# MLP up products of a hybrid encoder step: moving operand read in alternating pieces of 4 columns

## The reference

```python
h = _rmsnorm(x, norm2_g) * (1.0 + sc2) + sh2
x = x + g2 * (jnp.square(jax.nn.relu(h @ w_up)) @ w_down)
```

## Time and profile before

| what | us |
|---|---|
| median of 2 runs | 3328.43 |
| the two runs | 3326.7, 3330.15 |
| span of the profiled execution, first to last instruction | 3325.1 |
| TensorE busy in it | 3224.1 (97%) |
| VectorE busy | 1696.0 (51%) |
| ScalarE busy | 984.5 (30%) |
| GpSimd busy | 957.8 (29%) |

### The profile page before, as it was taken

One profiled execution on the slowest core, in us unless ns is written; L12 is line 12 of the kernel. 1 busy time (PEld: TensorE's weight loads), 2 busy tenths in 40 slices (PEclk: granted clock), 3 DMA queues, 4 the chain that ended last, 5 costly groups with the idle time before them and its releaser, 6 DMA issues.

```text
span 3325.1 us, 50329 instructions
## 1 busy us (share of the span) xinstructions
PE 3224.1 (97%) x19286; PEld 2894.2 (87%) x19286; DVE 1696.0 (51%) x3073; ACT 984.5 (30%) x1770; POOL 957.8 (29%) x690
## 2 busy tenths in 40 slices
PE   6999999899999999999999999999999999999998
PEld 3988897566799999999988879966678999999997
DVE  4746273674495555555573544156546633333335
ACT  3132222574451111111232313147635311111112
POOL 1312332221232333333332214212213233333332
PEclk8999999999999999999999999999999999999999
DMA  5512476535112222222222114563321011111112
GB/s 213 180 47 95 156 238 218 125 91 139 33 59 85 85 76 76 88 82 82 83 64 73 35 50 176 190 172 76 76 66 45 27 51 44 44 45 50 44 44 72
DMA packets 135351, 307.07 MB, mean 92 GB/s; under 512 B 53789, under 2 KB 74341, under 8 KB 131729
## 3 DMA queue, kind: packets, MB, share of 16 engines
q1 hardware_dynamic: 93584, 224.39, 23.4%
q10 hardware_dynamic: 41600, 80.44, 6.9%
HBM read 240.14 MB, written 57.90 MB: 90 GB/s over the span
## 4 chain that ended last, share of the span: by engine, by line
PE 90%; DVE 4%; SPq 2%; ACT 1%; ACTq 1%; issue 1%; DMA 1%; DVEq 0%
PE ps L1387 22%; PE ps L1358 19%; PE ps L1299 9%; PE ps L1232 8%; PE ps L1022 6%; PE ps L1212 5%; PE ps L1078 4%; PE ps L1169 3%; PE ps L1276 3%; PE ps L1004 2%; PE ps L1046 1%; DVE tn L2053 1%; PE ps L1334 1%; DVE h_lo L2066 1%; DVE x L2238 1%; PE ps L1113 1%
## 5 line engine op out<-in xcount | busy, mean ns | idle before, releaser
L768 POOL CAST w_hi<-raw 128x1024 fp32r<-128x1024 f32 x212 | 229.5, 1082 | 1862.5 <-PEq L1393 447.3
L2238 DVE SCALAR_TENSOR_TENSOR x<-ps,mod,x 128x352 f32<-128x352 f32 (+2 forms) x768 | 353.6, 489 | 431.5 <-PE ps L1387 351.5
L1387 PE MATMUL ps<-act_hi,w_hi 128*128 128x352 f32 x1536 | 496.0, 323 | 0.0
L1387 PE MATMUL ps<-act_hi,w_lo 128*128 128x352 f32 x1536 | 492.6, 321 | 0.0
L1387 PE MATMUL ps<-act_lo,w_hi 128*128 128x352 f32 x1536 | 492.1, 320 | 0.0
L1358 PE MATMUL ps<-h_hi,w_hi 128*128 128x352 f32 x1344 | 433.5, 323 | 0.0
L1875 ACT ACTIVATE relu_b<-ps,consts 128x352 f32<-128x352 f32 x192 | 106.4, 554 | 1103.5 <-PE ps L1358 1084.3
L1358 PE MATMUL ps<-h_hi,w_lo 128*128 128x352 f32 x1344 | 430.8, 320 | 0.0
L1358 PE MATMUL ps<-h_lo,w_hi 128*128 128x352 f32 x1344 | 430.4, 320 | 0.0
L1299 PE MATMUL ps<-pT,vb 128*128 128x512 f32 (+5 forms) x1080 | 401.3, 461 | 0.0
L2302 DVE TENSOR_REDUCE pm<-ps 128x1 f32<-128x512 f32 (+4 forms) x468 | 251.2, 548 | 243.3 <-PE ps L1169 158.8
(11 more groups left out here) (223 smaller groups left out, 6112.3 us busy)
## 6 DMA issues: line engine op xcount, KB each, us to landing
raw<-in_w SPq DMA_DIRECT2D x212, 512.0 KB, 3.6
ada_next<-in_w_ada SPq DMA_DIRECT2D x48, 512.0 KB, 4.2
ada_w<-in_w_ada SPq DMA_DIRECT2D x24, 512.0 KB, 5.9
kb<-scr_k SPq DMA_DIRECT2D x36, 328.0 KB
kb<-scr_k SPq DMA_DIRECT2D x120, 82.0 KB
qb<-scr_q SPq DMA_DIRECT2D x36, 264.0 KB
ada_nat<-in_w_ada_first SPq DMA_DIRECT2D x8, 1024.0 KB, 20.5
qb<-scr_q SPq DMA_DIRECT2D x120, 66.0 KB
```

The costliest lines, as they stand in the source:

```text
L768: pool.tensor_copy(hi, raw[:, uc % 2, 0:width]).then_inc(pool_hi, 1)
L1387: last = mm(ps[:, i % 6, 0:GW], w[:, k * 256 + o * 128:k * 256 + o * 128 + 128], (act_lo if low else act_hi)[:, k * T + g * GW:k * T + (g ...
L2238: last = v.scalar_tensor_tensor(xs, ps[:, bank, a - g * GW:b - g * GW], gs, xs, ALU.mult, ALU.add)
```

## The change

A constant STRAND = 4 is new. In `up`, the moving operand of each matmul, 352 contiguous columns, is seen as two halves a of 176 columns, each 44 pieces b of 4 columns c, and is read in the order b, a, c: four columns of the first half, four of the second, the next four of the first, and so on. The output is written through a pattern of the same order (b, a, c) over the bank's first 352 columns, which is one consecutive run of addresses. So the sum of input column a * 176 + b * 4 + c stands at b * 8 + a * 4 + c. The relu of `evict` reads PSUM in pieces that put the columns back and writes relu_b in the old order; it does so for the tiles of `up` only, and those of `up_first` are made and read as before.

```diff
--- before.py
+++ after.py
@@ -36,6 +36,7 @@
 PHASES = 5
 RET, OUT0, PROJ, ATT, MLP = range(PHASES)
 PRIME = 3
+STRAND = 4
 
 
 def rows(t):
@@ -1355,8 +1356,10 @@
                             pe.wait_ge(up_relu, n * 12 + (i - 6 + 1))
                         for k in range(KB):
                             for w, low in PASSES:
-                                last = mm(ps[:, i % 6, 0:GW], w[:, b % 2, k * 128:(k + 1) * 128],
-                                          (h_lo if low else h_hi)[:, k * T + g * GW:k * T + (g + 1) * GW],
+                                last = mm(ps[:, i % 6, 0:GW].rearrange("p (b a c) -> p b a c", a=2, c=STRAND),
+                                          w[:, b % 2, k * 128:(k + 1) * 128],
+                                          (h_lo if low else h_hi)[:, k * T + g * GW:k * T + (g + 1) * GW].rearrange(
+                                              "p (a b c) -> p b a c", a=2, c=STRAND),
                                           start=(k == 0 and w is w_hi and not low), stop=(k == KB - 1 and low == 1))
                         last.then_inc(up_ps, 1)
                         if g == 0:
@@ -1872,7 +1875,12 @@
                     act.wait_ge(sq_kept, n * 12 + (i - 1))
                 else:
                     act.wait_ge(up_lo, n * 12 + 1)
-                A(relu_b[:, i % 2, :], ps[:, UP_BANK[first][i], 0:GW], ACT.Relu, bias=zero).then_inc(up_relu, 1)
+                if first:
+                    A(relu_b[:, i % 2, :], ps[:, UP_BANK[first][i], 0:GW], ACT.Relu, bias=zero).then_inc(up_relu, 1)
+                else:
+                    A(relu_b[:, i % 2, :].rearrange("p (a b c) -> p a b c", a=2, c=STRAND),
+                      ps[:, UP_BANK[first][i], 0:GW].rearrange("p (b a c) -> p a b c", a=2, c=STRAND), ACT.Relu,
+                      bias=zero).then_inc(up_relu, 1)
                 act.wait_ge(up_relu, n * 12 + (i + 1))
                 A(act_hi[:, b * T + g * GW:b * T + (g + 1) * GW], relu_b[:, i % 2, :], ACT.Square, bias=zero).then_inc(up_hi, 1)
```

## The result

The changed kernel takes 3357.08 us (two runs, 3356.68 and 3357.48) against 3328.43 us: ratio 1.0086, 95% interval 1.0069 to 1.0104. That is no change by the 2% bound, and inside the stated range, but it is a real loss of 29 us where none was forecast.

The account below looks back on a forecast made before the run. TensorE's own products, busy 97% of the span, were taken as the bound. The parts summed 0 + 0 + 0 on the 3325.1 us span, with the median 3.3 us above it: 3328 us, range 3279 to 3475 for 8 in 10.

Parts of the forecast that it names:

- The bound and the place: TensorE's products bound the kernel; only the step of L1358, 159.0 ns, or a wait opening between products can change the time.
- the wait at the turn: From up to down, a slower relu has 2.0 us of cover before down's products wait; 0 on the path.
- part 1 of the sum: Moving read of the up products in pieces of 4: taken as 0, ends -50 us and +947 us.
- the likeliest case: No change beyond some ns a product, of either sign: chance 0.73, own range 3310 to 3350 us.
- The prediction's first sign: In the profile after, a chunk's chain must again read 45.8 us for 288 products of L1358.
- its bound for being wrong: The prediction is wrong if L1358's step leaves 159 ns by more than 16 ns, or a wait opens at the turn.
- A step before the sum: From L1169's contiguous reads: a column costs about one cycle, so the 12.3 ns above 146.7 is a charge per product.
- A smaller misreading: The two times, 3326.7 and 3330.15 us, were taken to lie 1.6 and 5.1 us above the execution's span of 3325.1.
- Rival A: Each of 87 jumps stalls the moving read one cycle: step 195 ns, 146 us more, 3475 us; chance 0.11.
- Rival B: The 12.3 ns is the moving read clashing with the next weight load; two slow streams avoid it: to 3279 us; chance 0.06.
- C: The relu reading pieces becomes the bound, if past 2.6 us; at 3.6 us it adds 14 us; no chance given.
- D: The pieces merge into one run, so the operand's order is not what the instruction reads; called impossible, no price.

Follow-up runs that it names:

- evict_only: Up products read as in the kernel before, only the relu behind them reads PSUM in pieces of 4; 3328.48 us, ratio 0.9997 to the kernel before.

## Why the prediction was right and wrong

**The bound and the place** were right. TensorE's step is all that moved; the eviction was free (evict_only), and the wait at the turn didn't open even where the square became 0.33 us longer. By the price of a ns, 4.03 us, 7.8 ns make 31.4 us, and the chunks of the chain add up to just that.

**The step that made the forecast miss** is part 1 of the sum, the moving read, "I take 0, the value that the nearest row has". It measured 7.8 ns a product, 31.4 us, and nothing else in the sum moved. The row was read rightly as far as a stream can tell: 384 columns cost 175.5 ns in three pieces and in one, and L1212's 177.2 ns, with pieces further apart, lies 1.7 ns above. But it was too far in shape. 7.8 ns lies inside the ends that were given, -12.3 and 235, and the likeliest case's own range, 3310 to 3350, allowed 5 ns on a product; it was too narrow by 7 us. The prediction's first sign, 45.8 us for 288 products, was missed by 2.2 us, while its bound for being wrong, 16 ns, was twice the change that came. The prediction thought in jumps only, and priced a jump. The runs show that 87 jumps can cost 1 ns (onward, at a step of 8) or 7.7 ns (the change) or 16 (192 apart), and that 43 can cost 8.7. Why pieces of 4 by turns cost what they do stays open.

**A step before the sum failed too**: "a column costs about one cycle and the 12.3 ns is a charge per product", so that another order of reading has nothing to cure. It was drawn from the earlier trace rows, two distances between starts known to 10 ns, which left 0.36 to 0.45 ns a column. Over the 146.7, 160.0 and 213.3 ns that 352, 384 and 512 columns last at 2.4 GHz, pairs take 2.5 ns each time, the contiguous read 12.3, 15.5 and 18.5 ns. So 2.5 of the 12.3 ns are paid once a product, and 9.8 belong to the order of reading. How they are spread over the columns isn't settled. A contiguous column costs (231.8 - 159.0) / 160 = 0.455 ns between 352 and 512, above even the 0.45, but (159.0 - 118.8) / 96 = 0.419 ns between 256 and 352, which is one cycle. The question "another order of reading might cure it" was asked and answered no; the runs answer yes.

**A smaller misreading**: 5.1 us do not lie around the span. That is the second time less the first execution's span; an execution's time is under 2 us above its own span in every run (3356.68 and 3354.9 in the changed kernel's). It moved nothing in the sum.

**Rival A**, a cycle for each jump, is refuted: 195 ns was forecast by it and 166.8 measured, and pieces of 8 are no cheaper. **Rival B** had its mechanism wrong and its end nearly right. Shorter weight loads shorten neither the contiguous step (160.7 ns) nor pieces of 4 (167.7), so nothing speaks for a clash with the weight load. The Trainium skill (TensorE: Matmul & The Clock Gate, "Step-by-step: what each phase is for") has two independent read ports for the two operands, and the trace agrees with it as far as these streams go. But an order of reading that takes the step to 149.2 ns exists, from two slow streams as B had it, with pieces of 1 and not of 4. **C** and **D** as said: the relu takes 556 ns, and the pieces were read as pieces.

The rule of the Trainium skill on lines of 16 bytes (SBUF — State Buffer, "Door 1: The DMA port swizzle") gave 0 for this part, where 7.8 ns were measured. The streams agree that the line is a unit: pieces that straddle one cost 231.1 ns in place of 166.7. They don't agree that two hits on a line are enough: every second column, two hits a line, costs 312 ns.

## What to carry to other kernels

A stream of fp32r products on contiguous columns takes 12 to 19 ns a product more than its columns last at 2.4 GHz (256 to 512 columns). Read the moving operand as pairs, one column from each half of the tile with both halves moving on by one, and 2.5 ns are left of that (149.2 ns for 352 columns, 162.5 for 384, 215.8 for 512), with the permutation undone in an eviction that has slack. At 256 columns the gain is 7.1 ns, 111.7 against 118.8. Don't do it in bf16, and don't take pieces of 2, 4 or 8. Before a term is set to zero from a row of another shape, put a stream of just that operation on the chip: one run with 27 streams settled more here than any argument from the kernel's trace.

## What the runs showed that was not expected

The fast form is narrow. Pairs at any distance tried from 16 to 1056 columns give 149.2 ns, pairs 2 apart 149.9; one column from each of four runs gives 186.7 ns, and pieces of 2 from two runs 225.7 ns. The same pairs in bf16 take 333.6 ns against 149.2 contiguous. And pieces of 4 at an onward step of 24 columns cost 221.0 ns, where steps of 28 and 12 cost 163.8 and 158.3.
